# One encoder layer on one core: 16-column low-rank tile, products of ones at the start, feed-forward groups of 8, 7, 7, halved last tile, transfers moved to SyncE

## What is computed

```python
h = _rmsnorm(x, g_mix)
qa, ka, va, qb, kb, vb, rb, a1, ga, gb = split(h @ w_in)     # a1: GATE_RANK = 16 columns
log_a = log_sigmoid(a1 @ w_a2 + b_a) / 16
oa = windowed attention of qa, ka, va (16 query heads, 4 key heads, sinks, distance bias)
ob, state = gated linear attention of qb, kb, vb, log_a (4 heads)
m = sigmoid(ga) * oa + sigmoid(gb) * (_rmsnorm(ob, g_ob) * silu(rb))
x = x + m @ w_out
h = _rmsnorm(x, g_ffn)
x = x + (silu(h @ w_gate) * (h @ w_up)) @ w_down             # D_FF = 2816 = 22 x 128
```

## Time and profile before

| | |
|---|---|
| time, median of 3 runs | 924.65 us (924.46 to 924.68) |
| profiled execution, its own time | 923.59 us |
| its span | 921.8 us |
| TensorE matmul busy | 883.1 us, 96% of the span |
| VectorE, ScalarE, GpSimd busy | 577.1, 416.4, 275.2 us |
| share of TensorE in the chain that ended last | 79% |
| share of VectorE in it | 12% |
| mean granted clock | 0.998 of full |
| weights read | 71.87 MB, 82 GB/s over the span |

### The profile page before, as it was taken

One profiled execution on the slowest core, in us unless ns is written; L12 is line 12 of the kernel. 1 busy time (PEld: TensorE's weight loads), 2 busy tenths in 40 slices (PEclk: granted clock), 3 DMA queues, 4 the chain that ended last, 5 costly groups with the idle time before them and its releaser, 6 DMA issues.

```text
span 921.8 us, 17225 instructions
## 1 busy us (share of the span) xinstructions
PE 883.1 (96%) x7051; PEld 849.3 (92%) x7051; DVE 577.1 (63%) x1112; ACT 416.4 (45%) x763; POOL 275.2 (30%) x161
## 2 busy tenths in 40 slices
PE   3999999999899999999999998999999999999997
PEld 2898999989898999899999998999999999999997
DVE  5682656574787445656546698984269983379742
ACT  5642533434455545454534575652146542155441
POOL 2443223122333322323234212225222235122351
PEclk9999999999999999999999999999999999999999
DMA  8323122222422222121207457864278863278522
GB/s 247 92 62 86 50 80 70 58 69 58 107 76 70 61 56 69 48 70 55 61 1 199 107 136 151 188 142 125 64 173 165 183 140 112 67 178 175 120 72 62
DMA packets 154293, 94.59 MB, mean 103 GB/s; under 512 B 4064, under 2 KB 145078, under 8 KB 154214
## 3 DMA queue, kind: packets, MB, share of 16 engines
q1 hardware_dynamic: 138246, 71.88, 27.5%
q0 software_dynamic: 9504, 17.31, 11.9%
q10 hardware_dynamic: 6464, 4.29, 1.7%
HBM read 71.87 MB, written 3.60 MB: 82 GB/s over the span
## 4 chain that ended last, share of the span: by engine, by line
PE 79%; DVE 12%; ACT 4%; DMA 2%; issue 2%; ACTq 1%; SPq 0%; DVEq 0%; POOLq 0%
PE G L596 15%; PE G L598 14%; PE G L597 14%; PE G L850 4%; PE G L852 4%; PE G L853 4%; PE X L850 4%; PE X L852 4%; PE X L853 4%; PE X L770 2%; DVE qAT L1589 2%; PE X L754 2%; PE X L739 1%; DVE rs L1389 1%; DVE rs L1390 1%
## 5 line engine op out<-in xcount | busy, mean ns | idle before, releaser
L596 PE MATMUL G<-h_hi,w_hi 128*128 128x272 f32 x1296 | 387.8, 299 | 6.7 <-DVE rv L1552 2.8
L598 PE MATMUL G<-h_hi,w_lo 128*128 128x272 f32 x1296 | 375.4, 290 | 0.0
L597 PE MATMUL G<-h_lo,w_hi 128*128 128x272 f32 x1296 | 373.2, 288 | 0.0
L545 POOL TENSOR_TENSOR w_lo<-wraw,w_hi 128x1024 fp32r<-128x1024 f32 x85 | 217.0, 2556 | 421.7 <-ACT w_hi L977 421.5
L596 PEld LDWEIGHTS G<-h_hi,w_hi 128*128 128x128 f32 x1296 | 244.4, 189 | 18.4 <-issue 13.6
L597 PEld LDWEIGHTS G<-h_lo,w_hi 128*128 128x128 f32 x1296 | 245.1, 189 | 0.6
L598 PEld LDWEIGHTS G<-h_hi,w_lo 128*128 128x128 f32 x1296 | 244.3, 188 | 0.0
L977 ACT ACTIVATE w_hi<-wraw 128x1024 fp32r<-128x1024 f32 x129 | 135.2, 1050 | 64.1 <-PE G L598 38.6
L1909 DVE TENSOR_TENSOR rs<-G,rv 128x544 f32<-128x544 f32 x24 | 17.4, 724 | 79.6 <-PE G L598 79.6
L1177 ACT ACTIVATE prob<-prob,nm 128x256 f32<-128x256 f32 (+2 forms) x80 | 36.7, 460 | 63.9 <-DVE sd L1621 63.9
L1308 ACT ACTIVATE sq<-sq 128x544 f32<-128x544 f32 x22 | 14.5, 659 | 101.5 <-DVE sq L1822 101.5
(11 more groups left out here) (302 smaller groups left out, 1815.1 us busy)
## 6 DMA issues: line engine op xcount, KB each, us to landing
wraw<-in_w_in_dram SPq DMA_DIRECT2D x53, 512.0 KB
wraw<-in_w_gate_dram SPq DMA_DIRECT2D x22, 512.0 KB
wraw<-in_w_up_dram SPq DMA_DIRECT2D x22, 512.0 KB
csum<-csum POOLq DMA_DIRECT2D x44, 256.0 KB, 5.1
wraw<-in_w_down_dram SPq DMA_DIRECT2D x16, 512.0 KB
wraw<-csum POOLq DMA_DIRECT2D x22, 256.0 KB, 3.3
wraw<-in_w_out_dram SPq DMA_DIRECT2D x8, 512.0 KB
wraw<-in_w_down_dram SPq DMA_DIRECT2D x8, 384.0 KB
```

The lines of the kernel that those rows point to most:

```text
L545: pool.tensor_tensor(w_lo[:, slot, :, :], wraw[:, slot, :, :], w_hi[:, slot, :, :].bitcast(F32), ALU.subtract).then_inc(w_split, 1)
L596: pe.matmul(o, w_hi[:, slot, kc, :], b_hi[:, kc, cols], start=(kc == 0), stop=False)
L597: pe.matmul(o, w_hi[:, slot, kc, :], b_lo[:, kc, cols], start=False, stop=False)
L598: mm = pe.matmul(o, w_lo[:, slot, kc, :], b_hi[:, kc, cols], start=False, stop=(kc == last))
```

## The change

1. Tile 0 (`a1`) has 16 columns instead of 128: the load, `high_part`, `low_part` and `chunk` take `m` columns.
2. `keep_busy`: TensorE makes 10 products of the 128 x 128 tile of ones with itself after the second transfer of x, and 11 more after VectorE's two row sums, before the first turn. The products are float32 with 128 columns and their results are not read.
3. The eight transfers of `keys_out` are issued by SyncE, after the load of tile 31.
4. The groups are 8, 7, 7, and `bank_set` shifts the alternation by one in groups 1 and 2: they begin on `X`, and the wait for `G` (`set_free`) moves to the group's second pair.
5. Around pairs 0 and 1: the last two `add_squares` follow `evict_7(0)`, `x2_squares` follows the addition into b7, `copy_p1(0)` stands before the square and `copy_p1(1)` before the first tanh, and VectorE runs `evict_6(1)` ahead of `gated(0)` and `evict_7(1)` right behind it.
6. The last down tile is scaled, added, turned, copied and sent in two parts, by ScalarE (rows 0 to 255) and by VectorE and SyncE (the rest); the sample rows of the other tiles are sent by SyncE.

```diff
-    tiles = [("a1", 0, [(O_A1, P)])]
+    tiles = [("a1", 0, [(O_A1, RANK)])]
...
-FF_GROUPS = [8, 8, 6]
+FF_GROUPS = [8, 7, 7]
...
+def bank_set(q):
+    g, _ = PAIRS[q]
+    return (q - FIRST[g] + (g > 0)) % 2
...
+            def keys_out():
+                sp.wait_ge(kt_out, 1)
+                sp.dma_start(nk_p[0, 0].rearrange("t h d -> t (h d)"), kout[:, 0, :]).then_inc(out_sem, 16)
+                sp.dma_start(nk_s[0, 0].rearrange("t h d -> t (h d)"), kout[0:DEC, 1, :]).then_inc(out_sem, 16)
+                for dst, src in ((kST, kAT), (kcS, kcT)):
+                    sp.dma_start(dst[0:HD, :, :], src[HD:P, :, :]).then_inc(k_swapped, 16)
+                    sp.dma_start(dst[HD:P, :, :], src[0:HD, :, :]).then_inc(k_swapped, 16)
...
+                if n == KEYS_OUT + 2 * RING:
+                    keys_out()
...
+            for i in range(KC - 1):
+                sp.wait_ge(y_ok, i + 1)
+                sp.dma_start(y_sample[0, :, i * P:(i + 1) * P], ytok[0:DEC, i % 2, SJ, :]).then_inc(y_out[i % 2], 16)
...
+            def keep_busy(ps, count):
+                for _ in range(count):
+                    pe.matmul(ps, ones[:, :], ones[:, :], start=True, stop=True)
             pe.wait_ge(const_pool, 1)
             pe.wait_ge(const_dve, 1)
+            pe.wait_ge(in_x[1], 16)
+            keep_busy(G[0][:, 640:640 + P], 10)
             pe.wait_ge(in_small, 16 * N_SMALL)
...
+            pe.wait_ge(x_sums, len(ROWS_DVE))
+            keep_busy(X[1][:, 0:P], 11)
...
-                if q >= 2:
+                if q == FIRST[g]:
+                    pe.wait_ge(evicted, 6 * q)
+                elif q >= 2:
                     pe.wait_ge(evicted, 6 * (q - 1))
...
-                if q == FIRST[g]:
+                if g >= 1 and q == FIRST[g] + 1:
                     for r in range(2):
                         pe.wait_ge(set_free[(n + r) % 2], uses_before(n + r))
...
-                x2_squares()
                 pe.wait_ge(evicted, 2)
                 product(b7, w_hi[:, r1, k2], w_lo[:, r1, k2], fb_hi[:, :, 4], fb_lo[:, :, 4], adds=True)
+                x2_squares()
...
+            def last_rows(n):
+                i, r = KC - 1, (KC - 1) % 2
+                for b in range(2):
+                    t = slice(b * TH, (b + 1) * TH)
+                    link(dve.tensor_tensor(rs[:, t], G[n % 2][:, 512 * b:512 * b + TH], rv[:, t], ALU.mult))
+                    dve.tensor_tensor(x2T[:, i, t], x2T[:, i, t], rs[:, t], ALU.add).then_inc(x_added, 1)
+                dve.wait_ge(yt_done, KC + 1)
...
-            add_squares(KC - 2)
-            add_squares(KC - 1)
...
+                    if q == 1:
+                        evict_6(q)
+                        gated(q - 1)
+                        dve.wait_ge(fa_ok, q)
+                        evict_7(q)
+                        low_parts(q + 1, 0)
+                        mid_low_part(q - 1)
+                        first_sum(q + 2)
...
+                    if q == 0:
+                        add_squares(KC - 2)
+                        add_squares(KC - 1)
```

106 lines of the change are left out of this document (63 added, 43 removed).

## The result

The changed kernel takes 911.82 us (median of 4 executions, 911.00 to 913.53), the kernel before on the same chip 924.66 us. The ratio is 0.986 (95% interval 0.9841 to 0.9879). The profiled execution took 912.38 us by its own time, of which 910.6 are the span: 11.2 us less than the profiled one of before. That difference of 11.2 is what a comparison of the two traces can explain.

The account below looks back on a forecast made before the run. TensorE, busy for 883.1 us, was taken as the bound, with its waits and half-clock stretches to gain. Terms 4.9 + 2.9 + 1.2 + 0 + 0.5 = 9.5 us, from 924.65 to 915.1 us; 8-in-10 range 911.9 to 919.4.

Parts of the forecast that it names:

- Start, 4.9 forecast: First turn of x and tile 0: earlier turn and full clock from the first chunk gain 4.9 us, bounds 2.8 and 5.5.
- The term for sixteen columns: Products of tile 0: 48 matmuls keep their step of 0.125 us, so 0 gain, bounds 0 and 0.5 us.
- both levels: Eleven products of ones before the first turn: they end between 13.8 us (full clock) and 16.1 us (half clock).
- Keys, 2.9 forecast: ScalarE's root behind the keys comes 3.0 us earlier without the transfer issues: gain 2.9 us, bounds 2.2 and 3.0.
- Pairs, 1.2 forecast: Pairs 0 and 1: pair 2 starts at 562.5 instead of 563.7 us, gain 1.2, bounds 2.8 gain and 0.3 loss.
- The second wait: Last product of pair 1: a wait of 1.9 us for c4_lo takes over from the one of 2.5 us.
- Groups, 0 forecast: Starts of groups 1 and 2: 0.5 us gained, 0.5 lost by late sums, together 0; bounds 1.6 gain, 2.8 loss.
- End, 0.5 forecast: Last output rows: the last transfer leaves SyncE near 919.2 instead of 919.71 us, gain 0.5 us, bounds 0 and 0.8.
- not free before 917.2: End: ScalarE is busy until 917.2 us, when it has issued the next to last prompt rows.
- more than forecast: Rival, 0.07: last rows of x land earlier, low parts keep their place, transfers for the sums speed up; 912.4 us.
- The clock did not stay at half: Rival, 0.11: the clock stays at half level until after the first turn, the start gains nothing; 920.0 us.
- 64-byte pieces: Rival, 0.01: tile 0's load of 1024 pieces of 64 bytes lands late and delays the first turn; 926.5 us.

Follow-up runs that it names:

- s_128: Changed kernel with the products of ones, but tile 0 loaded, split and multiplied with 128 columns: 916.05 us, ratio 0.993.
- experiment 3: Changed kernel without the 21 products of ones: 914.58 us, ratio 0.9903; or with them but tile 0 at 128 columns: 916.05 us, ratio 0.993.
- experiment 1: Changed kernel measured again twice, unaltered: 913.03 us, ratio 0.9887, and 913.16 us, ratio 0.9877.
- b_groups: Kernel before with the group change alone (8, 7, 7 and shifted bank sets): 921.95 us, ratio 0.9978.
- experiment 2: Changed kernel with the first turn of probabilities two row chunks later, run twice: 911.55 us, ratio 0.9865, and 911.15 us, ratio 0.986.
- experiment 4: Changed kernel with the eight key and value transfers issued by ScalarE again: 915.65 us, ratio 0.9902.

## Why the prediction was wrong in its size, and what held

The direction was right, and so were the mechanisms of the start, the keys and the pairs. The step that failed is that of the groups, put at 0 and measured at 1.7 us; the end was too small by 0.6; and the level of the first comparison moved by the sample.

- **Start, 4.9 forecast.** The profiled pair shows 5.2. Over the eleven profiles with this start the last turn of x begins at 24.5 us on the mean, in the two with the old start at 29.4 and 28.7: 4.2 to 4.9. The first turn at 14.4 and scalings of 0.47 us came as worked out. The loop at 1.47 instead of 1.57 us gave a little more: the narrow tile shortens the first step behind a turn by 0.09 us, shown by s_128. The term for sixteen columns, taken as 0 with a bound of 0.5, is 0.6 us (experiment 3), and not by 48 shorter steps: 5 of 6 stayed at 126 ns. The Trainium skill, page "TensorE: Matmul & The Clock Gate", section "LDWEIGHTS (loading the stationary operand)", has a load take time by its columns. The trace agrees for the loads themselves (0.09 us listed with 16 columns, 0.19 with 128), but the matmuls' step follows only behind a turn. On the eleven products the text was right to carry both levels: both occur, and with the slow one the first turn came at 15.6 to 15.9 us.
- **Keys, 2.9 forecast.** 2.9 in the traces and in the undone version.
- **Pairs, 1.2 forecast.** 1.1. The second wait came as said (1.8 for 1.9), and the clock stayed up in twelve of the thirteen profiles with this order.
- **Groups, 0 forecast: this step failed.** "Together 0" was half right in how it came about: both starts lost their wait (1.4 us each), and both second pairs got one. What they gave back was 0.7 us on the mean at group 1 and 1.4 at group 2, where 0.9 and 1.9 were forecast. The prediction took the end of `c_lo` as fixed by the earlier trace rows; in the first profile it ended 13.0 us behind pair 8's start instead of 11.9, so of the 1.4 us it followed 0.3. The wait for it was also not longer in group 2, as the prediction said, but 0.57 us against 0.85. And the prediction looked for what the smaller groups change only at a group's start. At the last group's end the first down tile waits for the last pair's low part, 0.9 us with 6 pairs and 0.14 with 7: the largest part of the error. In all 1.7 us, just outside the 1.6 that the text gave as a bound.
- **End, 0.5 forecast: mis-sized.** 1.1. The text counted from the earlier trace rows only to the end of the last issue and found it 0.5 us earlier. It is 0.6 earlier: 908.98 - 905.04 = 3.9 us behind the turn of tile 6's rows instead of 919.71 - 915.13 = 4.6. And the end then comes 1.6 us behind that issue instead of 2.1, for the same 32 rows. ScalarE, "not free before 917.2", did not bound it: that is 2.07 us behind the turn of tile 6's rows, and it was free after 906.81 - 905.04 = 1.77, since it no longer waits for the copy of the sample rows. The last rows went by VectorE and SyncE.
- **The level.** 9.5 were forecast, and with these two terms corrected 9.5 + 1.7 + 0.6 = 11.8 us, against a mean of 11.6 over three comparisons. The first comparison's 12.8 was in part luck. It holds three executions of four without a fall of the clock, where all thirteen have six, and its median is 1.2 to 1.3 us below those of the later two; its sample of the kernel before is 0.5 to 1.4 us above the four later ones. How much of the rest is sample can't be told closer. The ratios of experiment 1 give 914.2 and 913.3 us against 924.65, inside the range of the forecast, which the first comparison left by 0.1 us. The term of the groups stays wrong at any of these levels.

Of the rivals, "more than forecast" (912.4) was nearest, but not for its reasons: the low parts did not keep their place and the last rows of x did not land earlier; of its parts only the groups' gain came, by another way. The clock did not stay at half, and 64-byte pieces held nothing. The rule on small pieces that the prediction cites speaks of rates: the load of an eighth of the bytes was never on the path here, so no run shows whether it holds.

What stays open: why the wait of 1.9 us is followed by a fall in some executions and not in others of the same kernel, and whether the kernel before falls there as often. In its profile and that of b_groups it did not, but its executions have clocks of 0.993 to 0.998, and of the 17 beside b_groups the five at 0.993 or 0.994 take 926.0 to 926.3 us, the others 922.1 to 924.8; where those fell is not recorded. If it falls there less often, this takes part of the gain back, and none of the terms above has it.

## What to carry to other kernels

When work is regrouped, walk every boundary of a group, its end as well as its start: what the first consumer behind the group waits for is covered by as many steps as the group has members. A transfer at the end counts from where its issue stands in its queue to its landing; here splitting the issues over two engines was worth nearly as much (0.5 us) as splitting the work (0.6). And where a TensorE-bound kernel spreads by 2 to 3 us, look in several profiles for half-level stretches behind its waits, which were 1.7 to 2.8 us here: moving one step of a waiting engine's work by two chunks was worth as much here as a whole item of the change.

## What the runs showed of the hardware

- The granted clock fell to 0.5 for some 3.4 us behind waits of TensorE of 1.7 to 2.8 us, in some executions and not in others of the same kernel; behind the waits of 1.3 us or less that stand alone it was seen in no profile. A fall costs 1.5 us (experiment 2), or nothing that can be seen, as behind the keys (experiment 4).
- At the start the products of ones go from 0.43 to 0.22 us each at a time that differs between executions of the same kernel, in the changed kernel around the start of the eleven or only behind them, while the profile's granted clock reads 1.00 from the first: there the level is seen in the step alone.
- Some 0.8 us of the wait of 1.9 us came from one tiny operation, VectorE's maximum over 128 x 4 elements before the first probabilities. In the changed kernel's first profile it took 1.2 us and ended with GpSimd's subtraction of a tile (283.45 + 2.36 = 285.81 us):

```profile
284.63 1.20 DVE L1664 TENSOR_TENSOR mx<-mx,sinkb 128x4 f32<-128x4 f32 x1
```

```profile
283.45 2.36 POOL L579 TENSOR_TENSOR w_lo<-wraw,w_hi 128x1024 fp32r<-128x1024 f32 x1 [3.75 <-ACT w_hi L1027]
```

The twenty of this line have a median of 0.44 us and the shortest took 0.16. The eleven that took over 0.4 us all end within 0.03 us of the end of such a subtraction; the other nine lie outside one or start in its last 0.13 us. It is the same collision as that of the earlier trace rows, and the change removed only the one at the start. The Trainium skill, page "Advanced Engine Details and Errata", section "VectorE Performance Modes", notes that VectorE's second port is shared with GpSimd and that the two block each other in the modes that use it. These rows show the blocking, whichever mode each operation had.
